# RWKV level loop: every head's intermediates in the opposite partition half, update and score products taken in turn with others

## The chip, the core and the metric

One core of one Trainium2 chip runs the whole program. The metric is the time of one execution on the device in microseconds (us); lower is better.

## What is computed

One step of a two-layer encoder for 320 frames (a prompt of 256, which are 4 chunks of 64, and a sample of 64, chunk 4). The first layer mixes the frames by an RWKV-7 recurrence with 8 heads of 64 in parallel to gated linear attention (GLA) with 4 heads, then a dense SwiGLU. The second has HGRN2 and a top-2-of-8 expert SwiGLU. The change lies in the RWKV part:

```python
def rwkv7_recurrence(r, w, k, v, kk, a, s0):
    def step(s, inp):
        r_t, w_t, k_t, v_t, kk_t, a_t = inp
        sa = jnp.einsum('bhvk,bhk->bhv', s, kk_t)
        s = (s * w_t[:, :, None, :] - sa[..., None] * (kk_t * a_t)[:, :, None, :]
             + v_t[..., None] * k_t[:, :, None, :])
        return s, jnp.einsum('bhvk,bhk->bhv', s, r_t)
```

The kernel computes it by chunks of 64 frames: for each chunk and head it inverts a triangular 64x64 matrix of frame products, and then carries the 64x64 states from chunk to chunk.

## The kernel before, in words

A pair of heads shares the 128 partitions: one in partitions 0 to 63 (half 0), one in 64 to 127 (half 1); `par` is the half, `f` the pair (0 to 3), written f = 2i + e. A product of one head and one chunk is a 64x64 by 64x64 matmul in float32. It reads both operands from one half and may write to either half of PSUM, so it uses one of four corners of TensorE's array: two **straight** ones (half 0 to 0, 1 to 1) and two **crossing** ones (0 to 1, 1 to 0). The trace shows each product as two MATMUL records, so 5 chunks x 8 heads x 2 = 80 records for a product over all of them.

`turned_pairs` (product in L712) issues the products of a list of chunks: pairs with e = 0 straight, pairs with e = 1 moved by its arguments `from_` and `to`, which say whether the odd heads' operands and result lie in the other half. With 0, 1 or 1, 0 two straight products alternate with two crossing ones. With 1, 1 all are straight. `diag` (L696) is straight always. The places, in the order of the program on TensorE (PE):

- `grams` (from L836): frame products of the chunks; kind "t" (three groups of 2, 2 and 1 chunks, 32, 32 and 16 records) by `turned_pairs` 0, 1; the others straight (L696, L856).
- `tm` transposes, GLA values and keys (L696, L772, L856).
- The level loop, `pe.Fori(1, LEVELS)`, 5 rounds over one body. `HALVES` splits the 5 chunks in two groups, [0, 1, 2] and [3, 4]. A round is X = At x Tm (L902, `turned_pairs` 0, 1) for both groups, then the GLA level's 20 straight score products (`level_scores`, L734), then for each group Y = Tt x Xm (L912; 1, 0) and Yt = Xm x Tt (L918; 1, 1). Round 0's Tm and Tt come from the grams.
  VectorE (DVE) multiplies X by a mask into Xm (L1731), copies the scores by mask (L1612) and makes the next level's GLA operand (L1644, L1645, L1639). ScalarE (ACT) copies Y to Tm (L2638) and Yt to Tt (L2640), and makes GLA exponentials (L2561, L2562). PE waits for the Xm of a group ahead of its Y (`inv_x`), for the scores' copy ahead of group 1's Yt, which is written into the same banks 6 and 7 (`gla_sc`), for the copy of Y ahead of the next X (`inv_y`), and for that of Yt of group 1 ahead of the scores (`inv_ready`).
- The steps, [0, 4], [1], [2], [3]: PE makes W1 (`w1`) from G1 and the carried state, last scores (step 0 alone, L761), the outputs' first two parts (`bo`), then U = Tt x W1, then TK x V (L696) into the state update `dh`, then the next step's W1 from G1. It waits for ACT's copy of U (L2659) and adds TQ x U to `dh` (`each`, L696) and G2 x U to the output. DVE copies W1 (L1765) ahead of U, and updates the state (L1784, L1785) behind `dh`; the next step waits for it. All but the L696 ones go by `turned_pairs` (L712).
- `rows_back` (L991): the output's rows by a product with the identity, odd f crossing, then GLA outputs (L805), ACT and DVE copies and the dense products of the output projection (L609, L613).

```python
                a_, z_ = par ^ (e & from_), par ^ (e & to)
                src, dst = slice(64 * a_, 64 * a_ + 64), slice(64 * z_, 64 * z_ + 64)
```

The remaining time (dense and expert SwiGLU) is dense float32 products split in two parts; the change doesn't touch it.

Of the kernel before, what the change touches and what calls it, by code (L numbers as in the profile page):

```python
# [75 lines left out]
def mixed_trunk(nc, ins, outs):  # L76
    ctx = ExitStack()
    with ctx:
# [154 lines left out]

        HALVES = [[0, 1, 2], [3, 4]]
        LAST = LEVELS - 1
# [317 lines left out]
        def _(pe):  # L553
# [138 lines left out]
            def diag(b, col, left, right, start, stop):  # L692
# [5 lines left out]
                return mm  # L698

            def turned_pairs(two, chunks, left, right, from_, to, start, stop):  # L700

                for j, c in enumerate(chunks):
                    for i in range(RF // 2):
                        for e in range(2):
                            l_, r_ = left(c, 2 * i + e), right(c, 2 * i + e)
                            if l_ is None:
                                continue
                            for turn_ in range(2):
                                par = turn_ ^ (e & from_ & to)
                                a_, z_ = par ^ (e & from_), par ^ (e & to)  # L710
                                src, dst = slice(64 * a_, 64 * a_ + 64), slice(64 * z_, 64 * z_ + 64)
                                mm = pe.matmul(two[dst, e, (2 * j + i) * C:(2 * j + i + 1) * C], l_[src], r_[src],  # L712
                                               start=start and j == 0 and i == 0, stop=stop and c == chunks[-1] and i == 1,
                                               skip_group_check=True)
                return mm
# [11 lines left out]

            def level_scores(two):

                for m_ in range(2 * NCH):  # L730
                    c, f = m_ // 2, m_ % 2
                    for par in range(2):
                        rows = slice(64 * par, 64 * par + 64)
                        mm = pe.matmul(two[rows, m_ // NCH, m_ % NCH * C:m_ % NCH * C + C], gla["Z"][rows, f, chunk(c)],  # L734
                                       gla["Z"][rows, f, chunk(c)], start=m_ % NCH == 0, stop=m_ % NCH == NCH - 1,
                                       skip_group_check=True)
                return mm

# [155 lines left out]
            def waited():  # L894

                pe.sem_inc(S("level_waited"), 1)

            with pe.Fori(1, LEVELS) as lv:
                for g, chunks in enumerate(HALVES):
                    pe.wait_ge(S("inv_y"), level_count(lv - 1, g))  # L900
                    waited()
                    turned_pairs(where["X", 1, g], chunks, lambda c, f: At[:, c, f, :], lambda c, f: Tm[:, c, f, :],  # L902
                                 0, 1, True, True).then_inc(S("inv_full"), 1)
                pe.wait_ge(S("inv_ready"), level_count(lv - 1, len(HALVES) - 1))
                pe.wait_ge(*at_count("gla_z", lv + 1))
                waited()
                pe.wait_ge(*first_done)
                level_scores(where["gla_sc", 1]).then_inc(S("gla_sc_full"), 1)
                for g, chunks in enumerate(HALVES):
                    pe.wait_ge(S("inv_x"), level_count(lv - 1, g))  # L910
                    waited()
                    turned_pairs(where["Y", 1, g], chunks, inverse_at, product_at, 1, 0, True, True).then_inc(S("inv_full"), 1)  # L912
                    if g == len(HALVES) - 1:
                        pe.wait_ge(*at_count("gla_sc", lv + 2))
                        waited()
                    else:
                        pe.wait_ge(*grams_done)
                    turned_pairs(where["Yt", 1, g], chunks, product_at, inverse_at, 1, 1, True, True).then_inc(S("inv_full"), 1)  # L918
            for g in range(len(HALVES)):
                for k in YT_AT[g]:  # L920
                    owner[k] = ("inv_ready", level_count(LAST, g))

            pe.wait_ge(*at_count("h_init", 1))
# [26 lines left out]
            for i, step in enumerate(STEPS):  # L950
# [23 lines left out]
                else:  # L974
                    gla_keys(w1_at)
                pe.wait_ge(*at_count("u_done", i + 1))
                each(dh, step, lambda c, f: TQ[:, c, f, :], lambda c, f: U[:, PLACE[c], f, :], False, True).then_inc(S("seq_full"), 1)
                turned_pairs(bo, step, lambda c, f: G2[:, c, f, :], lambda c, f: U[:, PLACE[c], f, :], 0, 1, False, True)\
                    .then_inc(S("seq_full"), 1)
            gla_updates()  # L980
# [2283 lines left out]
```

## Time and profile before

| | |
|---|---|
| time, median of 3 runs | 1468.73 us (1468.45 to 1468.87) |
| time of the profiled execution | 1469.37 us |
| its span | 1467.7 us |
| granted clock of TensorE, mean | 0.995 |
| busy PE, DVE, ACT | 97%, 80%, 65% |
| chain that ended last, by engine | PE 88%, DVE 7%, ACT 3% |
| stretch that the change touches | about 120 to 208 us |

The table is to be read from below: the change lies in one twentieth of the span, all of it in stretches at full granted clock, and the rest follows in the same order.

### The profile page before, as it was taken

What the parts mean: (1) busy time and instruction counts of PE and PEld (TensorE: products, weight loads), DVE (VectorE), ACT (ScalarE), POOL (GpSimd) and SP (SyncE); (2) the same over time, 40 slices, a digit from 0 to 9 for tenths busy, and PEclk for the clock granted to TensorE, in tenths of its full rate; (3) what the DMA queues carried; (4) which work ended last, traced back from release to release, by engine and by line L of the source; (5) the groups of instructions that cost most, each with busy time, mean ns of one, the idle gap of its engine ahead of it and who ended that gap; (6) DMA issues with size and microseconds to landing.
All of it is one profiled execution on the core that took longest, in us unless ns stands there. A gap on an engine that the chain in (4) does not pass through costs nothing.

```text
span 1467.7 us, 29198 instructions
## 1 busy us (share of the span) xinstructions
PE 1428.1 (97%) x11253; PEld 1278.1 (87%) x11254; DVE 1173.1 (80%) x1580; ACT 950.7 (65%) x1257; POOL 76.3 (5%) x152
## 2 busy tenths in 40 slices
PE   7999989999999999999999999999999999999997
PEld 7999988999999899888788888888888888888884
DVE  5686579545535789867998998899988999898997
ACT  4465455433323696476778787778777887877873
POOL 8300000000000000000000000000000000000000
PEclk9999999999999999999999999999999999999999
DMA  8431004544445262217999999999999999999992
GB/s 261 152 106 37 2 15 145 173 144 145 150 143 164 88 187 88 88 59 285 339 390 397 402 394 398 347 396 380 371 397 350 407 379 362 397 353 410 390 345 93
DMA packets 162214, 371.62 MB, mean 253 GB/s; under 512 B 10232, under 2 KB 85968, under 8 KB 162128
## 3 DMA queue, kind: packets, MB, share of 16 engines
q1 hardware_dynamic: 159352, 361.18, 67.2%
q0 software_dynamic: 2160, 7.87, 2.0%
q8 instruction: 61, 1.00, 0.3%
q10 hardware_dynamic: 616, 1.37, 0.2%
q14 instruction: 25, 0.20, 0.0%
HBM read 360.68 MB, written 9.71 MB: 252 GB/s over the span
## 4 chain that ended last, share of the span: by engine, by line
PE 88%; DVE 7%; ACT 3%; issue 1%; DMA 1%; SPq 0%; DVEq 0%; ACTq 0%
PE psum L1371 11%; PE psum L1372 11%; PE psum L1373 11%; PE psum L596 10%; PE psum L598 9%; PE psum L597 9%; PE psum L1395 5%; PE psum L1397 5%; PE psum L1396 5%; PE psum L712 2%; PE psum L1380 1%; PE psum L696 1%; PE psum L1133 1%; DVE wd_lo L1468 1%; PE psum L609 1%
## 5 line engine op out<-in xcount | busy, mean ns | idle before, releaser
L2184 DVE TENSOR_TENSOR w_lo<-moe_ring,w_hi 128x1024 fp32r<-128x1024 f32 (+1 forms) x560 | 608.3, 1155 | 28.9 <-ACT w_hi L2916 28.9
L2916 ACT ACTIVATE w_hi<-moe_ring 128x1024 fp32r<-128x1024 f32 (+1 forms) x560 | 531.6, 1015 | 69.4 <-PE psum L1397 39.0
L1371 PE MATMUL psum<-w_hi,xe_hi 128*128 128x512 f32 (+1 forms) x768 | 288.1, 375 | 1.6 <-DVE w_lo L2184 1.4
L1372 PE MATMUL psum<-w_hi,xe_lo 128*128 128x512 f32 (+1 forms) x768 | 285.9, 372 | 0.0
L1373 PE MATMUL psum<-w_lo,xe_hi 128*128 128x512 f32 (+1 forms) x768 | 285.4, 372 | 0.0
L1468 DVE TENSOR_TENSOR wd_lo<-arena,wd_hi 128x1024 fp32r<-128x1024 f32 x141 | 169.9, 1208 | 132.9 <-ACT wd_hi L2441 132.6
L596 PE MATMUL psum<-in_hi,wd_hi 128*128 128x320 f32 x800 | 250.5, 313 | 2.5 <-DVE wd_lo L1468 1.2
L2441 ACT ACTIVATE wd_hi<-arena 128x1024 fp32r<-128x1024 f32 (+1 forms) x140 | 146.2, 1047 | 157.4 <-PE psum L598 151.8
L598 PE MATMUL psum<-in_hi,wd_lo 128*128 128x320 f32 x800 | 247.2, 309 | 0.0
L597 PE MATMUL psum<-in_lo,wd_hi 128*128 128x320 f32 x800 | 247.1, 309 | 0.0
L1371 PEld LDWEIGHTS psum<-w_hi,xe_hi 128*128 128x128 f32 x768 | 144.5, 188 | 28.4 <-DVE w_lo L2184 2.9
L1373 PEld LDWEIGHTS psum<-w_lo,xe_hi 128*128 128x128 f32 x768 | 144.2, 188 | 25.8
L1372 PEld LDWEIGHTS psum<-w_hi,xe_lo 128*128 128x128 f32 x768 | 144.5, 188 | 24.9
L596 PEld LDWEIGHTS psum<-in_hi,wd_hi 128*128 128x128 f32 x800 | 150.1, 188 | 5.7 <-issue 1.8
L597 PEld LDWEIGHTS psum<-in_lo,wd_hi 128*128 128x128 f32 x800 | 150.2, 188 | 0.4
L598 PEld LDWEIGHTS psum<-in_hi,wd_lo 128*128 128x128 f32 x800 | 150.2, 188 | 0.0
L1395 PE MATMUL psum<-w_hi,gt_hi 128*128 128x512 f32 x256 | 101.3, 396 | 0.2 <-DVE w_lo L2184 0.2
L1397 PE MATMUL psum<-w_lo,gt_hi 128*128 128x512 f32 x256 | 99.7, 389 | 0.0
L1396 PE MATMUL psum<-w_hi,gt_lo 128*128 128x512 f32 x256 | 99.7, 389 | 0.0
L596 PE MATMUL psum<-hid_hi,wd_hi 128*128 128x320 f32 x224 | 69.7, 311 | 1.3 <-DVE wd_lo L1468 1.3
L598 PE MATMUL psum<-hid_hi,wd_lo 128*128 128x320 f32 x224 | 69.1, 309 | 0.0
L597 PE MATMUL psum<-hid_lo,wd_hi 128*128 128x320 f32 x224 | 69.1, 309 | 0.0
(449 smaller groups left out, 1799.5 us busy)
## 6 DMA issues: line engine op xcount, KB each, us to landing
moe_ring<-in_moe_w SPq DMA_DIRECT2D x216, 1024.0 KB, 8.8
moe_ring<-in_moe_w SPq DMA_DIRECT2D x64, 768.0 KB, 5.7
arena<-in_ffn_w SPq DMA_DIRECT2D x30, 1024.0 KB, 5.3
arena<-in_w_in_c SPq DMA_DIRECT2D x16, 1024.0 KB, 5.5
arena<-in_w_in_ab SPq DMA_DIRECT2D x12, 1024.0 KB, 5.5
arena<-in_w_out_ab SPq DMA_DIRECT2D x4, 1024.0 KB, 5.1
arena<-in_w_out_c SPq DMA_DIRECT2D x4, 1024.0 KB, 5.0
arena<-in_ffn_w SPq DMA_DIRECT2D x4, 768.0 KB, 4.3
```

Source lines behind the costliest of these rows:

```text
L596: pe.matmul(b[:, 0:T], w_[0][:, cols], x_hi, start=start, stop=False)
L597: pe.matmul(b[:, 0:T], w_[0][:, cols], x_lo, start=False, stop=False)
L598: return pe.matmul(b[:, 0:T], w_[1][:, cols], x_hi, start=False, stop=stop)
L1371: pe.matmul(b[:, 0:w], xe_hi[:, k, :], hi_[:, c0:c1], start=(k == 0), stop=False)
L1372: pe.matmul(b[:, 0:w], xe_lo[:, k, :], hi_[:, c0:c1], start=False, stop=False)
L1373: mm = pe.matmul(b[:, 0:w], xe_hi[:, k, :], lo_[:, c0:c1], start=False, stop=(k == KC - 1))
L1395: pe.matmul(E_Y[half][:, :], g_hi[:, g], hi_[:, cols], start=first, stop=False)
L1396: pe.matmul(E_Y[half][:, :], g_lo[:, g], hi_[:, cols], start=False, stop=False)
L1397: mm = pe.matmul(E_Y[half][:, :], g_hi[:, g], lo_[:, cols], start=False, stop=final)
L1468: dve.tensor_tensor(wd_lo[:, m_ % DENSE_UNITS, 0:words], src, rounded_of(m_)[:, 0:words], ALU.subtract).then_inc(S("dense_lo"), 1)
L2184: dve.tensor_tensor(w_lo[:, i % UNITS, 0:unit_words(i)], moe_unit(i), w_hi[:, i % UNITS, 0:unit_words(i)], ALU.subtract)\
L2916: act.activation(w_hi[:, i % UNITS, 0:unit_words(i)], moe_unit(i), ACT.Copy).then_inc(S("e_hi"), 1)
```

## The change

`turned` is now one product, and with `from_` or `to` 1 the operands or the result lie in the other half for every head, not the odd ones alone. So a product with 0, 1 or 1, 0 is all crossing, one with 1, 1 all straight. Groups of the levels are [0, 1] and [2, 3, 4].

In the level body X of group 0 and the first half of X of group 1 stand alone; then PE waits for `inv_ready` and `gla_z`, and the other 12 products of group 1 are taken in turn with the 20 scores: 2 crossing, then 2 or 4 scores. Y and Yt of a group are taken in turn, 2 and 2; so the wait for the scores' copy stands ahead of group 1's Y too. In the steps the product TQ x U and G2 x U are taken in turn, one and one. The rest of the steps, "t" of the grams and `rows_back` keep their place and turn all crossing.

```diff
-        HALVES = [[0, 1, 2], [3, 4]]
+        HALVES = [[0, 1], [2, 3, 4]]
...
+            def turned(two, chunks, head, left, right, from_, to, start=True, stop=True):
+
+                j, c, i, e, par = head
+                a_, z_ = par ^ from_, par ^ to
+                src, dst = slice(64 * a_, 64 * a_ + 64), slice(64 * z_, 64 * z_ + 64)
+                return pe.matmul(two[dst, e, (2 * j + i) * C:(2 * j + i + 1) * C], left(c, 2 * i + e)[src], right(c, 2 * i + e)[src],
+                                 start=start and j == 0 and i == 0, stop=stop and c == chunks[-1] and i == 1, skip_group_check=True)
...
+                heads, scored = chunk_heads(HALVES[1]), 0
+                alone = len(heads) // 2
+                for head in heads[:alone]:
+                    turned(where["X", 1, 1], HALVES[1], head, product_of, before_at, 0, 1)
                 pe.wait_ge(S("inv_ready"), level_count(lv - 1, len(HALVES) - 1))
...
+                for n, head in enumerate(heads[alone:]):
+                    mm = turned(where["X", 1, 1], HALVES[1], head, product_of, before_at, 0, 1)
+                    if n == alone - 1:
+                        mm.then_inc(S("inv_full"), 1)
+                    if n % 2:
+                        until = 2 * ((n + 1) * scores // (2 * alone))
+                        for m_ in range(scored, until):
+                            score = level_score(where["gla_sc", 1], m_)
+                        scored = until
+                score.then_inc(S("gla_sc_full"), 1)
                 for g, chunks in enumerate(HALVES):
                     pe.wait_ge(S("inv_x"), level_count(lv - 1, g))
                     waited()
-                    turned_pairs(where["Y", 1, g], chunks, inverse_at, product_at, 1, 0, True, True).then_inc(S("inv_full"), 1)
                     if g == len(HALVES) - 1:
                         pe.wait_ge(*at_count("gla_sc", lv + 2))
...
+                    for head, other in zip(heads[::2], heads[1::2]):
+                        for h_ in (head, other):
+                            y = turned(where["Y", 1, g], chunks, h_, inverse_at, product_at, 1, 0)
+                        if other == heads[-1]:
+                            y.then_inc(S("inv_full"), 1)
+                        for h_ in (head, other):
+                            yt = turned(where["Yt", 1, g], chunks, h_, product_at, inverse_at, 1, 1)
...
-                each(dh, step, lambda c, f: TQ[:, c, f, :], lambda c, f: U[:, PLACE[c], f, :], False, True).then_inc(S("seq_full"), 1)
-                turned_pairs(bo, step, lambda c, f: G2[:, c, f, :], lambda c, f: U[:, PLACE[c], f, :], 0, 1, False, True)\
-                    .then_inc(S("seq_full"), 1)
+                for head in chunk_heads(step):
+                    j, c, i_, e, par = head
+                    f, rows = 2 * i_ + e, slice(64 * par, 64 * par + 64)
+                    o = (RF * j + f) * C
+                    state = pe.matmul(dh[rows, o:o + C], TQ[rows, c, f, :], U[rows, PLACE[c], f, :], start=False,
+                                      stop=c == step[-1] and f == RF - 1, skip_group_check=True)
+                    if head == chunk_heads(step)[-1]:
+                        state.then_inc(S("seq_full"), 1)
+                    out = turned(bo, step, head, lambda c, f: G2[:, c, f, :], lambda c, f: U[:, PLACE[c], f, :], 0, 1, False, True)
...
-                            a_ = par ^ (f % 2)
+                            a_ = par ^ 1
```

On PE, the body of the level loop, before: L712 are the products of X (24 and 16), of Y and Yt (64, 16), L734 the scores.

```order
L898 ISA
L712 MATMUL psum<-arena 64x64 x24
L900 REGISTER_ALU
L712 MATMUL psum<-arena 64x64 x16
L905 REGISTER_ALU
L734 MATMUL psum<-arena 64x64 x20
L712 MATMUL psum<-arena 64x64 x64
L914 REGISTER_ALU
L712 MATMUL psum<-arena 64x64 x16
```

The same body now: L709 are the products of `turned`, L736 the scores. L913 stands at the wait for `gla_z`, L930 at that for the scores' copy.

```order
L709 MATMUL psum<-arena 64x64 x16
L905 REGISTER_ALU
L709 MATMUL psum<-arena 64x64 x12
L913 REGISTER_ALU
L709 MATMUL psum<-arena 64x64 x2
L736 MATMUL psum<-arena 64x64 x2
L709 MATMUL psum<-arena 64x64 x2
L736 MATMUL psum<-arena 64x64 x4
...
L736 MATMUL psum<-arena 64x64 x4
L709 MATMUL psum<-arena 64x64 x32
L930 REGISTER_ALU
L709 MATMUL psum<-arena 64x64 x48
```

The counts are the same, 120 and 20. X has moved into the scores, group 1 has 48 products behind the wait for the scores' copy where 16 stood behind it, and group 0 has 32 ahead of it.

On PE, the end of step 1, before (L696 are TK x V and TQ x U, the first L712 the next step's W1, the last G2 x U and what follows):

```order
L712 MATMUL psum<-arena 64x64 x48
L696 MATMUL psum<-arena 64x64 x8
L712 MATMUL psum<-arena 64x64 x8
L696 MATMUL psum<-arena 64x64 x8
L712 MATMUL psum<-arena 64x64 x40
```

And now (L1007 is TQ x U):

```order
L709 MATMUL psum<-arena 64x64 x33
L696 MATMUL psum<-arena 64x64 x8
L709 MATMUL psum<-arena 64x64 x8
L1007 MATMUL psum<-arena 64x64
L709 MATMUL psum<-arena 64x64
L1007 MATMUL psum<-arena 64x64
L709 MATMUL psum<-arena 64x64
L1007 MATMUL psum<-arena 64x64
```

The 8 products TQ x U no longer stand ahead of the 8 of G2 x U, but alternate with them; W1, output and U products keep their place and number.

## Rows read from the trace of the kernel before

**Rows 1.** The page: busy time, and the chain that ended last.

```profile
PE 1428.1 (97%) x11253; PEld 1278.1 (87%) x11254; DVE 1173.1 (80%) x1580; ACT 950.7 (65%) x1257; POOL 76.3 (5%) x152
...
PE 88%; DVE 7%; ACT 3%; issue 1%; DMA 1%; SPq 0%; DVEq 0%; ACTq 0%
```

**Rows 2.** The chain in order of time, 126 to 196 us: start, us, what.

```profile
126.70 0.14 issue
126.84 0.69 PE psum L712 x32
...
129.66 8.70 PE psum L696 x296
...
150.10 0.71 issue
...
180.00 0.39 issue
...
190.65 0.95 DVE stat L1738
```

**Rows 3.** Timeline, PE: start, us, group, [idle before <-releaser].

```profile
126.84 0.69 PE L712 MATMUL psum<-arena 64*64 64x64 f32 x32 [0.54 <-DVE arena L1705]
...
129.96 7.21 PE L696 MATMUL psum<-ident,arena 64*64 64x64 f32 x240
...
186.84 0.93 PE L712 MATMUL psum<-arena 64*64 64x64 f32 x48 [0.75 <-DVE arena L1785]
```

**Rows 4.** Timeline of the third and fourth rounds, all engines.

```profile
160.34 4.92 PE L712 MATMUL psum<-arena 64*64 64x64 f32 x238
...
161.31 0.81 ACT L2638 ACTIVATE arena<-psum 128x768 f32<-128x768 f32 x1 [1.80 <-PE psum L712]
...
162.67 0.81 ACT L2640 ACTIVATE arena<-psum 128x768 f32<-128x768 f32 x1 [0.56 <-PE psum L712]
...
164.07 0.60 ACT L2640 ACTIVATE arena<-psum 128x512 f32<-128x512 f32 x1
...
164.85 1.55 DVE L1731 TENSOR_TENSOR arena<-psum,lower 128x768 f32<-128x768 f32 x2 [2.06 <-PE psum L712]
...
165.05 1.30 PE L734 MATMUL psum<-arena 64*64 64x64 f32 x38
...
166.22 4.92 PE L712 MATMUL psum<-arena 64*64 64x64 f32 x238
...
166.45 0.56 DVE L1612 COPY_PREDICATED arena<-upper,psum 128x160 f32<-128x160 int32 x2
```

**Rows 5.** DVE timeline, first round's copy of the scores.

```profile
147.59 0.89 DVE L1612 COPY_PREDICATED arena<-upper,psum 128x160 f32<-128x160 int32 x2
```

**Rows 6.** Groups by shape, 144.8 to 177.6 us: busy us, mean ns.

```profile
L1731 DVE TENSOR_TENSOR arena<-psum,lower 128x768 f32<-128x768 f32 x5 | 4.8, 958 | 9.0 <-PE psum L712 9.0
...
L1731 DVE TENSOR_TENSOR arena<-psum,lower 128x512 f32<-128x512 f32 x5 | 3.4, 680 | 0.0
L1639 DVE TENSOR_TENSOR arena<-arena 128x640 f32<-128x640 f32 x4 | 3.3, 824 | 0.1
L2638 ACT ACTIVATE arena<-psum 128x768 f32<-128x768 f32 x4 | 3.2, 811 | 11.9 <-PE psum L712 11.9
```

**Rows 7.** Timeline, steps 1 and 2 and the head of step 3.

```profile
182.85 1.80 PE L712 MATMUL psum<-arena 64*64 64x64 f32 x63 [0.85 <-DVE arena L1785]
...
183.92 0.58 PEld L712 LDWEIGHTS psum<-arena 64*64 64x64 f32 x15 [0.29 <-DVE arena L1765]
...
185.18 0.62 PE L696 MATMUL psum<-arena 64*64 64x64 f32 x14
```

**Rows 8.** Timeline, step 2: U, TK x V, TQ x U.

```profile
187.92 0.55 PE L712 MATMUL psum<-arena 64*64 64x64 f32 x14
...
188.21 0.27 PE L696 MATMUL psum<-arena 64*64 64x64 f32 x2
188.25 0.28 PE L712 MATMUL psum<-arena 64*64 64x64 f32 x2
...
189.00 0.62 PE L696 MATMUL psum<-arena 64*64 64x64 f32 x14
```

**Rows 9.** Timeline, `rows_back` and the GLA outputs behind it.

```profile
197.93 0.96 PE L991 MATMUL psum<-ident,arena 64*64 64x64 f32 x46
...
198.82 2.45 PE L805 MATMUL psum<-arena 64*128 64x64 f32 x40
...
201.20 0.69 PE L991 MATMUL psum<-ident,arena 64*64 64x64 f32 x32
```

More of the change, by code:

```diff
@@ L698, in diag, with chunk_heads @@
                 return mm
-            def turned_pairs(two, chunks, left, right, from_, to, start, stop):
[L702 to L714, printed above, removed]
+            def chunk_heads(chunks):
+                return [(j, c, i, e, par) for j, c in enumerate(chunks) for i in range(RF // 2) for e in range(2) for par in range(2)]
+            def turned(two, chunks, head, left, right, from_, to, start=True, stop=True):
[4 more added lines that the diff above has]
+                                 start=start and j == 0 and i == 0, stop=stop and c == chunks[-1] and i == 1, skip_group_check=True)
+            def turned_pairs(two, chunks, left, right, from_, to, start, stop):
+                for head in chunk_heads(chunks):
+                    _, c, i, e, _ = head
+                    if left(c, 2 * i + e) is not None and right(c, 2 * i + e) is not None:
+                        mm = turned(two, chunks, head, left, right, from_, to, start, stop)
                 return mm
@@ L726, in _, with level_score @@
                   .then_inc(S("gate_full"), 1)
[L728 to L737, printed above, removed]
+            def level_score(two, n):
+                m_, par = n // 2, n % 2
+                c, f = m_ // 2, m_ % 2
+                rows = slice(64 * par, 64 * par + 64)
+                return pe.matmul(two[rows, m_ // NCH, m_ % NCH * C:m_ % NCH * C + C], gla["Z"][rows, f, chunk(c)],
+                                 gla["Z"][rows, f, chunk(c)], start=m_ % NCH == 0, stop=m_ % NCH == NCH - 1, skip_group_check=True)
             def first_scores():
@@ L896, in waited @@
                 pe.sem_inc(S("level_waited"), 1)
+            product_of = lambda c, f: At[:, c, f, :]
+            before_at = lambda c, f: Tm[:, c, f, :]
+            scores = 4 * NCH
             with pe.Fori(1, LEVELS) as lv:
[L899 to L903, printed above, removed]
+                pe.wait_ge(S("inv_y"), level_count(lv - 1, 0))
+                waited()
+                turned_pairs(where["X", 1, 0], HALVES[0], product_of, before_at, 0, 1, True, True).then_inc(S("inv_full"), 1)
+                pe.wait_ge(S("inv_y"), level_count(lv - 1, 1))
+                waited()
+                heads, scored = chunk_heads(HALVES[1]), 0
+                alone = len(heads) // 2
+                for head in heads[:alone]:
+                    turned(where["X", 1, 1], HALVES[1], head, product_of, before_at, 0, 1)
                 pe.wait_ge(S("inv_ready"), level_count(lv - 1, len(HALVES) - 1))
+                waited()
                 pe.wait_ge(*at_count("gla_z", lv + 1))
@@ L907, in _ @@
                 pe.wait_ge(*first_done)
-                level_scores(where["gla_sc", 1]).then_inc(S("gla_sc_full"), 1)
+                for n, head in enumerate(heads[alone:]):
[8 more added lines that the diff above has]
+                score.then_inc(S("gla_sc_full"), 1)
                 for g, chunks in enumerate(HALVES):
@@ L917, in _ @@
                         pe.wait_ge(*grams_done)
-                    turned_pairs(where["Yt", 1, g], chunks, product_at, inverse_at, 1, 1, True, True).then_inc(S("inv_full"), 1)
+                    heads = chunk_heads(chunks)
+                    for head, other in zip(heads[::2], heads[1::2]):
[5 more added lines that the diff above has]
+                            yt = turned(where["Yt", 1, g], chunks, h_, product_at, inverse_at, 1, 1)
+                    yt.then_inc(S("inv_full"), 1)
             for g in range(len(HALVES)):
@@ L921, in _ @@
                     owner[k] = ("inv_ready", level_count(LAST, g))
+            for k in Y_AT[0]:
+                owner[k] = ("inv_full", inverse_count("Y", LAST, 0))
             pe.wait_ge(*at_count("h_init", 1))
@@ L976, in _ @@
                 pe.wait_ge(*at_count("u_done", i + 1))
-                each(dh, step, lambda c, f: TQ[:, c, f, :], lambda c, f: U[:, PLACE[c], f, :], False, True).then_inc(S("seq_full"), 1)
-                turned_pairs(bo, step, lambda c, f: G2[:, c, f, :], lambda c, f: U[:, PLACE[c], f, :], 0, 1, False, True)\
-                    .then_inc(S("seq_full"), 1)
+                for head in chunk_heads(step):
[7 more added lines that the diff above has]
+                    out = turned(bo, step, head, lambda c, f: G2[:, c, f, :], lambda c, f: U[:, PLACE[c], f, :], 0, 1, False, True)
+                out.then_inc(S("seq_full"), 1)
             gla_updates()
```

## The prediction

> **What bounds the kernel now.** I read the page first. TensorE is busy 97% of the span, and the chain that ended last runs over PE for 88% of it [rows 1]. So time that PE gains or loses on that chain goes to the end. The chain in order of time [rows 2] shows where: from 126.84 to 181 us it is PE almost alone, interrupted by two pieces of "issue", 0.71 us at 150.10 and 0.39 at 180.00, where PE waits for nothing that the trace names. From there the steps alternate between PE, DVE and ACT, and from 195.8 PE carries it again. So most of the touched stretch has no slack, and the question is how fast PE gets through these small products.
>
> Next, how fast each kind of product is. 240 records of straight products take 7.21 us with the last one's own 0.22 in it: 6.99 / 239 = **29.2 ns each** [rows 3]. 48 records of `turned_pairs` 0, 1, two straight and two crossing in turn, take 0.93: 0.71 / 47 = **15.1 ns each** [rows 3]. The size is the same, so it is the corners: four in use go twice as fast as two. A second reading within one round says the same. Between ACT's start on Y of group 0 (161.31) and on its Yt (162.67) lie 48 straight records, 1.36 us; between its start on Yt of group 1 (164.07) and DVE's on X (164.85) lie 48 mixed ones, 0.78 [rows 4]. No stretch of before has crossing products alone. They use two corners, one per half, as the straight ones do. From below they can't beat 15.1, which four corners need, from above nothing is known. I take 29.2, since a corner in the mixed stretch (a record each 4 x 15.1 = 60 ns) and one in the straight stretch (2 x 29.2 = 58) have the same speed of their own: the number of corners in use decides.
>
> Per 16 records (one chunk) a product that turns from mixed to crossing alone costs 16 x 14.1 ns = 0.23 us, if PE is on the chain there.
>
> **The levels.** PE's own time of a round now: X and Y mixed, 160 x 15.1 = 2.42; Yt and scores straight, 120 x 29.2 = 3.50; sum 5.92. The trace has 166.22 - 160.34 = 5.88 [rows 4], so nothing but PE limits a round. After the change: X of group 0 alone 32 x 29.2 = 0.93; half of X of group 1 24 x 29.2 = 0.70; the rest with the scores, where the 40 straight score records on two corners last longest, 1.17; Y and Yt in turn, 160 x 15.1 = 2.42. Sum 5.22, a gain of **0.66 to 0.7 a round**, 3.4 in five.
>
> Against it stand the waits, which were covered before and now are not. PE may begin Y and Yt of group 1 only when the scores are copied. Behind the end of X of group 1 come the mask product over three chunks, 0.96 [rows 6], and the two score copies, 0.57 (0.90 in the first two rounds) [rows 4, 5], and about 0.05 of signals: 1.55 us (1.85). PE has work for 1.1 in that time: the last scores, some 0.15 past the signal, and Y and Yt of group 0, 64 x 15.1 = 0.97. It **waits 0.45 (0.8)**. Second, X of group 1 needs ACT's copy of Y of three chunks, 0.81 [rows 6] and about 0.25 of signals, against 0.93 of X of group 0: 0.14 more in four rounds. So a round is 5.22 + 0.45 + 0.14 = 5.8 (three times) and 6.15 (twice): -0.2 and +0.5. **Levels: +0.2 us**, from -3.4 (waits hidden) to +1.4 (X ends only with the scores). The next operand's chain on DVE (L1644, L1645, L1639 0.82 [rows 6]) starts behind the copies and has over 2 us; I cost it at nothing. The 0.71 of issue stands in the first round [rows 2] and I leave it.
>
> How far X of group 1 ends ahead of the scores rests on products overtaking each other. The trace shows it: two L696 records start at 188.21, the two L712 records that stand ahead of them in the program at 188.25 and after [rows 8]; corners have queues of their own. The Trainium skill (TensorE: Matmul & The Clock Gate, The mechanism) says otherwise, that matmuls start and end strictly in program order. By it X would end some 0.1 us later in each round, and the levels come to +0.7; the trace decides here.
>
> **Grams "t".** 32 records of the second group and 16 of the third turn crossing on the chain: +0.68. The first group's 32 lie ahead of 0.54 us in which PE waits for DVE [rows 3], which hides their 0.45. **+0.7.**
>
> **Step 0** is PE's alone: W1 32 + 16, output 32 + 16, U 32, next W1 16: 144 records x 14.1 = 2.03. Where a crossing batch meets a straight one they overlap by a record or two per corner; I take **+1.9**. The taking in turn of TQ x U and G2 x U brings nothing: 32 straight records alone last 0.93, 64 mixed 0.97, and DVE waits for the end of the straight ones either way. Against this, the issue at 180.00 (0.39) is time from fetching; with PE slower in front of it, it should go: **-0.4**, from 0.
>
> **Steps 1 and 2.** From the state's arrival to U PE needs 1.07 (182.85 to 183.92 [rows 7]): W1, DVE's copy, and in its shade the output's parts. Now W1 and both parts are 48 crossing records, 1.40, which outlasts W1 and its copy (0.5 + 0.23 + 0.53 = 1.26): +0.33 each. From U to TQ x U it took 1.26 (to 185.18 [rows 7]) and 1.08 (187.92 to 189.00 [rows 8]). Now 48 records, U, TK x V and W1, 1.40 less some 0.15 of overlap: 1.25, so 0 and +0.17. **+0.8**, from +0.5 to +1.5.
>
> **Step 3.** DVE's normalization, which starts at 190.65 with the state of step 2 [rows 2], holds the chain until 194.9, and PE's 0.5 of delay fits nearly into it: **+0.1**, up to +0.5.
>
> **rows_back.** 48 records took 0.75 to 0.86, now 1.40; 32 took 0.69 with 0.22 of tail, now 0.93 without it [rows 9]; PE's GLA outputs follow at once: +0.54 and +0.46, **+1.0**, from +0.5.
>
> Sum: 0.2 + 0.7 + 1.9 - 0.4 + 0.8 + 0.1 + 1.0 = **+4.3 us**. The profiled execution took 1469.37; with it 1473.7. The median of the runs is 0.64 lower, so the forecast is **1473.0 us**, 0.3% slower. In short: the level loop's gain is eaten by its waits, while all products that lost their straight neighbours pay in full.
>
> **Rivals.** (a) The forecast, with its own range of 1470.5 to 1475.5: 0.55.
> (b) The waits of the levels are hidden, and the whole 3.4 is gained. For it speaks that DVE is idle 9.0 us ahead of L1731 [rows 6]; against it that this idleness lies elsewhere in the round. 1473.0 - 3.6 = 1469.4, no change: 0.17.
> (c) The update products hinder each other. Now each TQ product is followed by a G2 product from the same half, in the order 0-0, 0-1, 1-1, 1-0, an order that no row of before has. If two products from one half don't overlap, 64 records cost 29.2 rather than 15.1 ns, and the state comes at their end: 0.9 in step 0, 0.45 in each of steps 1 and 2, up to 0.5 in step 3: +2.3, 1475.3, slower: 0.19. Against it: the mixed batches have four corners, hence two of one half, at work at once. The Trainium skill (same page and section) has a rule for it: a weight load overlaps with running matmuls only where the row group differs, by which these neighbours would lose the overlap.
> (d) The other side. Crossing products alone run at 15.1, so no product pays and X costs 0.47 and 0.35 instead of 0.93 and 0.70. Then all terms but the levels' are 0, and the levels need 4.4 a round plus waits: nearly the whole difference turns into waits if the copies are the limit (-0.5), none if they are covered (-7.5). It decides from half of that on: about -4, 1464.7, faster: 0.09. Against it speaks the equal speed of a corner in both kinds of batch.
>
> **How the numbers follow.** A measurement of this kernel can tell about 0.2%, 2.9 us, from no change. Slower by more: most of (a), 0.46, and (c), 0.19: 0.65. Within: the rest of (a) and (b): 0.26. Faster: (d), 0.09. The range leaves out (d) and takes in (b) below, and above the sum of (c) and the upper ends of two or three terms: 1468.8 to 1478.0.
>
> **What would show it.** In the changed kernel's trace: crossing batches alone at 29 ns a record (X of group 0: 32 records in 0.93 plus tail); Y and Yt in turn at 15; PE idle 0.4 to 0.8 us a round ahead of Y of group 1, released by DVE's L1612; rounds of 5.8 and 6.1 us; step 0 longer by 1.5 to 2; "issue" at its end gone; steps 1 and 2 of 4.3 us each; L991's 48 and 32 records at 29 ns each. The forecast falls if a crossing batch goes at 15 ns, if rounds take 5.2, or if PE isn't what the steps wait for.

## The result, and the profile after

| | before | after |
|---|---|---|
| median of the runs, us | 1468.66 (11 runs, 1468.19 to 1470.67) | 1472.66 (11 runs, 1470.96 to 1474.27) |
| profiled execution, its own time | 1469.37 | 1472.96 |
| its span | 1467.7 | 1471.2 |

The ratio is **1.0029, 95% interval 1.0021 to 1.0037**: slower by 4.0 us of the medians. The forecast was 1473.0 and "slower". The total came out within 0.4 us, but its terms did not: the levels were forecast too low, the grams and step 0 too high, and these errors nearly cancel.

The page of after answers to [rows 1]. Nothing in it tells of the change: PE is the bound as before, with the same share of the chain.

```profile
PE 1428.6 (97%) x11253; PEld 1278.3 (87%) x11254; DVE 1173.0 (80%) x1580; ACT 950.2 (65%) x1257; POOL 75.8 (5%) x152
...
PE 88%; DVE 7%; ACT 3%; issue 1%; DMA 1%; SPq 0%; DVEq 0%; ACTq 0%
```

So I cut the touched stretch into stages by marks that both kernels have: PE's start on the first L856 record (121.18 before, 120.74 after), DVE's start on the fifth product with the mask of G1 (145.26, 144.79), ACT's start on the last copy of Yt (175.83, 177.02), PE's start after each state update, and PE's start on L613 behind the outputs (207.77, 211.33). This is the view by windows; first before, then after:

```profile
core 0: us, PE busy (x) PEld busy (x) DVE busy (x) ACT busy (x) POOL busy (x), PEclk, DMA share, GB/s
121.18:145.26 24.08, 23.54 (x659) 23.07 (x662) 17.01 (x37) 13.47 (x26) 0.00 (x0) 1.00 0.02 4
145.26:175.83 30.57, 29.86 (x1414) 29.71 (x1408) 19.86 (x36) 14.62 (x26) 0.00 (x0) 1.00 0.00 1
175.83:207.77 31.94, 26.40 (x893) 24.33 (x883) 21.56 (x46) 14.80 (x31) 0.00 (x0) 1.00 0.02 4
```

```profile
120.74:144.79 24.05, 23.43 (x657) 22.97 (x658) 17.02 (x36) 13.48 (x26) 0.00 (x0) 1.00 0.02 4
144.79:177.02 32.23, 28.29 (x1397) 27.08 (x1395) 19.83 (x36) 13.86 (x25) 0.00 (x0) 1.00 0.00 1
177.02:211.33 34.31, 28.78 (x897) 27.36 (x894) 21.67 (x46) 14.92 (x31) 0.00 (x0) 1.00 0.01 3
```

The three stages together last 86.59 us before and 90.59 after. That is 4.0, as much as the medians differ. The spans of these two executions differ by 3.5, because the part ahead of the stretch happens to be 0.44 shorter in the second; behind the stretch they agree within 0.1. So no loss lies outside the stretch. The granted clock is 1.00 in all six rows. The middle pair is the interesting one. In the levels PE was busy 1.57 us less (29.86 to 28.29), as the change intends, and yet the stage is 1.66 longer (30.57 to 32.23): PE was idle for 0.71 of it, and is now for 3.94: 3.03 of it ahead of Y of group 1 and 0.90 of "issue". In the third stage PE has simply more to do, 2.38, and the stage is 2.37 longer.

**The levels.** Timeline of after: PE's starts on Y of group 1 in the first two rounds, then the third and fourth rounds on all engines; [rows 4] stood for these before.

```profile
149.00 1.11 PE L709 MATMUL psum<-arena 64*64 64x64 f32 x58 [0.79 <-DVE arena L1645]
...
156.21 3.83 PE L709 MATMUL psum<-arena 64*64 64x64 f32 x154 [0.79 <-DVE arena L1645]
...
162.57 3.83 PE L709 MATMUL psum<-arena 64*64 64x64 f32 x154 [0.48 <-DVE arena L1645]
...
167.31 1.15 PE L709 MATMUL psum<-arena 64*64 64x64 f32 x59
...
167.37 0.96 DVE L1764 TENSOR_TENSOR arena<-psum,lower 128x768 f32<-128x768 f32 x1 [1.15 <-PE psum L709]
168.25 0.55 DVE L1645 COPY_PREDICATED arena<-upper,psum 128x160 f32<-128x160 int32 x2
...
168.94 1.63 PE L709 MATMUL psum<-arena 64*64 64x64 f32 x96 [0.49 <-DVE arena L1645]
170.59 0.81 ACT L2671 ACTIVATE arena<-psum 128x768 f32<-128x768 f32 x1 [1.08 <-PE psum L709]
...
170.76 2.01 PE L709 MATMUL psum<-arena 64*64 64x64 f32 x58 [0.19 <-issue]
```

Each round has two holes. The first is the forecast one: at 167.37 X of group 1 is done and DVE takes the mask product over three chunks (L1764, 0.96), then the two copies of the scores (L1645, 0.55), and PE starts Y of group 1 at 168.94, 1.57 later. It has the 59 records at 167.31 to do in that time, whose last starts at 168.24. So PE starts nothing for 0.70 us, of which 0.49 shows as idle behind the last record's end. In the first two rounds, where the copies take 0.86, it starts nothing for 1.01, of which 0.79 shows as idle. The second hole was not in the forecast. Between the 96 records of Y and Yt and the next round's X lie 0.19 of "issue", 0.15 to 0.17 in the other rounds; PE waits for nothing that the trace shows. It lies where the loop's body ends and begins anew: the loop's turn. There 0.36 to 0.41 lies between two starts.

By DVE's starts on X of group 1 (161.00 and 167.37) this round lasts 6.37, the next one too. It was 5.88, and 5.8 was forecast. The first two last 7.21 and 6.67, where 6.15 was forecast; before they took 7.10 and 5.88.

**The rates.** The first row is a crossing batch alone, the row at 168.94 above Y and Yt in turn:

```profile
126.39 0.97 PE L709 MATMUL psum<-arena 64*64 64x64 f32 x26 [0.62 <-DVE arena L1738]
127.15 0.27 PE L696 MATMUL psum<-arena 64*64 64x64 f32 x2
127.17 0.28 PE L709 MATMUL psum<-arena 64*64 64x64 f32 x3
```

(0.97 - 0.22) / 25 = 30 ns a record, and (1.63 - 0.22) / 95 = 14.8 ns. Both are what the corners said, 29.2 and 15.1 [rows 3]. These rows also show records of the later straight batch (L696) starting at 127.15, before the crossing ones ahead of them in the program (127.17) have all begun, as in [rows 8]. The batch at 126.39 has 32 records, 0.93 us at 29.2 ns, and the next one begins after 0.76: **a join of a crossing and a straight batch hides 0.17 us**.

**The steps and the outputs**, chain of waits in order of time; [rows 2, 7] were the steps before, [rows 9] the outputs.

```profile
184.89 1.91 PE psum L709 x58
...
189.15 1.91 PE psum L709 x58
...
193.40 1.91 PE psum L709 x58
...
200.94 1.06 PE psum L1024 x37
202.00 2.38 PE psum L805 x40
204.38 1.08 PE psum L1024 x32
```

At the head of each step the chain now runs for 1.91 us over crossing records without a break: W1, both parts of the outputs and U. Before, it ran over W1 alone (16 records, 0.51) and DVE's copy, and the outputs stood beside it. Steps 1 and 2 last 4.25 each (184.89, 189.15, 193.40). In `rows_back` (L1024) the chain holds 1.06 and 1.08 where it held 0.74 and 0.62 on L991, the same line before.

All stages, after and in the experiments below (us, from the same marks):

| | grams | levels | step 0 | step 1 | step 2 | step 3 | outputs | sum |
|---|---|---|---|---|---|---|---|---|
| before | 24.07 | 30.57 | 7.02 | 3.99 | 3.83 | 5.13 | 11.97 | 86.59 |
| after | 24.05 | 32.23 | 7.87 | 4.25 | 4.25 | 5.17 | 12.75 | 90.59 |
| e1_groups | 24.05 | 29.32 | 7.87 | 4.25 | 4.25 | 5.17 | 12.75 | 87.66 |
| e2_y_apart | 24.05 | 34.46 | 7.81 | 4.25 | 4.25 | 5.17 | 12.75 | 92.76 |
| e3_scores_apart | 24.05 | 31.50 | 7.87 | 4.25 | 4.25 | 5.17 | 12.75 | 89.84 |
| e4_update_apart | 24.05 | 32.01 | 7.92 | 4.24 | 4.23 | 5.17 | 12.75 | 90.37 |
| e5_out_mixed | 24.05 | 32.02 | 7.53 | 4.11 | 4.11 | 5.13 | 11.97 | 88.92 |
| e6_groups_mixed | 24.05 | 29.36 | 7.72 | 4.11 | 4.10 | 5.13 | 11.97 | 86.43 |
| e7_early_scores | 24.05 | 29.65 | 7.71 | 4.11 | 4.11 | 5.13 | 11.97 | 86.73 |
| e8_pairs | 24.04 | 29.29 | 7.19 | 4.11 | 4.11 | 5.13 | 11.98 | 85.85 |
| e9_turn | 24.05 | 30.04 | 6.99 | 4.11 | 4.11 | 5.13 | 11.97 | 86.39 |

Stages that an edit doesn't touch repeat within 0.05 us, except "levels" and "step 0", where pieces of "issue" differ (by 0.2 in the levels of after against e4 and e5). Each row is one execution. The time of a whole run is coarser: the stretch itself begins anywhere from 119.3 to 121.5 us in these executions. So the stages carry the reading, and the ratio of the runs is its check.

### The profile page after: what moved, and what is told of

The parts are those of the page before. It is cut to its first block, busy times and chain, and to the rows that moved or that the text cites. A ratio compares the mean times of both kernels' runs of the same rounds, so it can differ in the third digit from the quotient of the medians.

```text
span 1471.2 us, 29204 instructions
## 1 busy us (share of the span) xinstructions
PE 1428.6 (97%) x11253; PEld 1278.3 (87%) x11254; DVE 1173.0 (80%) x1580; ACT 950.2 (65%) x1257; POOL 75.8 (5%) x152
## 3 DMA queue, kind: packets, MB, share of 16 engines
q0 software_dynamic: 2160, 7.87, 2.0%
## 4 chain that ended last, share of the span: by engine, by line
PE 88%; DVE 7%; ACT 3%; issue 1%; DMA 1%; SPq 0%; DVEq 0%; ACTq 0%
PE psum L1404 11%; PE psum L1405 11%; PE psum L1406 11%; PE psum L596 9%; PE psum L597 9%; PE psum L598 9%; PE psum L1428 5%; PE psum L1430 5%; PE psum L1429 5%; PE psum L709 2%; PE psum L1413 1%; PE psum L1166 1%; DVE wd_lo L1501 1%; PE psum L696 1%; PE psum L609 1%
```

## Experiments

Each edit is to the changed kernel or to the experiment named. A ratio is to the kernel before, run on the same chip, whose median was 1468.16 for e1 to e4, 1468.20 for e5 to e7 and 1467.79 for e8 and e9.

### e1_groups: three and two chunks again

```diff
-        HALVES = [[0, 1], [2, 3, 4]]
+        HALVES = [[0, 1, 2], [3, 4]]
```

> The changed kernel with the old groups, [0, 1, 2] and [3, 4]. Theory A (the waits of the levels eat their gain: after X of group 1 the mask product and the scores' copy take longer than PE has work): the mask product of group 1 shrinks from 0.96 to 0.68 us and Y with Yt of group 0 grow from 64 to 96 records, 0.97 to 1.45 us, so the wait ahead of Y of group 1 (PE idle 0.48 to 0.79 us a round in the changed kernel) disappears and a round falls from 6.37 to about 5.7 us; the kernel becomes 3 to 4 us faster than the changed one, about level with the kernel before. Rival B (the exposed time is the loop's own turn and the products' rate, whatever the groups): rounds stay at 6.2 or more, gain under 1 us.

Measured: 1471.26 us, ratio 1.0013 (1.0004 to 1.0022). The levels went from 32.23 to 29.32, the later rounds from 6.37 to 5.84, nothing else moved. By the ratios the kernel is some 2.3 us faster than the changed one, not 3 to 4, and by the interval not quite level with the kernel before: rounds of 5.7 were expected, and the loop's turn makes the difference. The chain of waits holds no DVE piece any more, only that turn:

```profile
160.11 2.51 PE psum L709 x156
162.62 0.15 issue
162.77 2.02 PE psum L709 x62
...
165.95 2.48 PE psum L709 x156
168.43 0.15 issue
```

With group 0 of three chunks PE has 96 records, 1.4 us, to do while the scores are copied, and the mask product ahead of the copies is one of two chunks. With the old groups the wait is hidden.

The stage of 29.32 is 1.25 us below before's 30.57, but little of this lies in the repeated rounds: they last 5.87, 5.84 and 5.81 against 5.88. By DVE's starts on X of group 1 the stage begins 0.84 slower, the first round is 0.57 shorter, the other three 0.12 together, and what stands behind the last X 1.40 shorter. There, in the last round, Y and Yt in turn gain over 1 us, and no turn follows. In a repeated round 0.47 less of PE's work (80 x 14.1 = 1.13 gained by Y and Yt, 64 x 14.1 = 0.90 lost by X alone, 16 x 15.1 = 0.24 gained by X among the scores) stands against 0.33 for the turn. So even with the wait hidden a round gains next to nothing.

### e2_y_apart: Y, then Yt

```diff
+                    turned_pairs(where["Y", 1, g], ..., 1, 0, True, True).then_inc(S("inv_full"), 1)
...
-                    for head, other in zip(heads[::2], heads[1::2]):
...
+                    turned_pairs(where["Yt", 1, g], ..., 1, 1, True, True).then_inc(S("inv_full"), 1)
```

The edit does two things: Y of group 1 also stands ahead of the wait for the scores' copy again, as before the change.

> The changed kernel, Y and Yt of a group one after the other again. PE's own time of a round grows by 160 x 14.1 ns = 2.3 us if a crossing batch and a straight batch next to each other don't overlap; theory A with overlapping joins (about 0.23 us hidden at each change between crossing and straight, two products per corner in the queue): four joins hide up to 0.9 and the two waits (0.7 and 0.36 us a round) are covered, so a round is about 6.4 to 6.8 us and the kernel 0 to 2 us slower than the changed one. Without overlap at the joins: 7.3 us a round, 4 to 5 us slower.

Measured: 1474.39 us, ratio 1.0036 (1.0024 to 1.0048). The levels take 34.46, 2.2 more than after, and behind the first round (0.49 of "issue") PE has no idle piece in the levels:

```profile
160.56 5.89 PE L709 MATMUL psum<-arena 64*64 64x64 f32 x209
...
167.40 5.83 PE L709 MATMUL psum<-arena 64*64 64x64 f32 x209
```

A round by these two starts is 6.84. Worked out at 29.2 ns for every record but those with the scores it would be X 0.93 + 0.70, scores 1.17, Y and Yt 160 x 29.2 = 4.67, together 7.47. The starts of single records in the trace show where the missing 0.63 lies. In a round there are four places at which some 12 records start 15 ns apart instead of 29: from the scores to Y, from Y to Yt, from Yt to Y, from Y to Yt (160.4, 161.1, 161.9 and 163.1 us). Each hides 0.17, 0.68 together: the later batch begins before the earlier one has started all its records, as at 127.15 above. The fifth place, the loop's turn from Yt to X at 164.4, hides nothing; its 16 records take 0.09 more than 16 x 29.2 ns. Together 7.47 - 0.68 + 0.09 = 6.88.

So the turn no longer shows as idle, but it isn't free: against a join inside the body it costs 0.26.

### e3_scores_apart: X alone, then the scores

```diff
-                    if n % 2:
-                        until = 2 * ((n + 1) * scores // (2 * alone))
-                        for m_ in range(scored, until):
-                            score = level_score(where["gla_sc", 1], m_)
-                        scored = until
+                for m_ in range(scores):
+                    score = level_score(where["gla_sc", 1], m_)
```

> The changed kernel, X of group 1 whole and then the scores. If the wait for the scores' copy (counted from the end of X of group 1) sets the round, X ends 1 us earlier in the round's order and PE's extra 24 records x 29.2 = 0.70 us replace the wait of 0.70: rounds stay at 6.3 to 6.4 us and the time within 0.5 us of the changed kernel's. If PE's own work sets it: 0.7 us more a round, 3.5 us slower.

Measured: 1472.36 us, ratio 1.0024 (1.0015 to 1.0034). Rounds of 6.31 against 6.37, and 6.73 and 6.54 in the first two against 7.21 and 6.67. Taking X and the scores in turn saves PE 0.7 a round and gains nothing here: X of group 1 ends earlier in e3, the copies are done in time, and PE idles 0.14 in two rounds and not at all in the others. What was won by the turns was given back as the wait, and a little more: the levels of 31.50 are 0.5 shorter than the 32.01 and 32.02 of e4 and e5, whose level body is that of after. The sum agrees: X 2.34 + scores 1.17 + Y and Yt 2.42 + the turn 0.36 = 6.29.

### e4_update_apart: TQ x U, then G2 x U

```diff
-                for head in chunk_heads(step):
...
-                    out = turned(bo, step, head, ..., 0, 1, False, True)
-                out.then_inc(S("seq_full"), 1)
+                each(dh, step, ..., False, True).then_inc(S("seq_full"), 1)
+                turned_pairs(bo, step, ..., 0, 1, False, True).then_inc(S("seq_full"), 1)
```

> The changed kernel, TQ x U whole and then G2 x U. My account: the alternation neither gains nor costs on the chain, since DVE waits for the last TQ product either way (16 straight records 0.47 us, 32 mixed 0.48): steps 1 and 2 stay at 4.25 us each, the time within 0.5 us of the changed kernel's. Rival (neighbours from one half hinder each other): steps shorter by 0.2 to 0.45 us each, 0.9 in step 0, 1 to 2 us faster.

Measured: 1471.52 us, ratio 1.0020 (1.0010 to 1.0029). The steps don't change, 4.23 and 4.24 by the chain of waits:

```profile
185.37 1.91 PE psum L709 x58
...
189.60 1.91 PE psum L709 x58
...
193.84 1.91 PE psum L709 x58
```

In step 0 of after the records of TQ x U and G2 x U in turn start 15 ns apart (182.4 to 183.3 us), the rate of four corners. The ratio of whole runs is 0.0009 lower than after's, 1.3 us, more than the 0.5 expected and within what rival (c) would give; but the two intervals overlap, and the stretch is only 0.22 shorter, all of it in the levels. So neighbours from the same row half don't hinder each other here, and taking these two in turn brings nothing either.

### e5_out_mixed: the outputs' products mixed again

```diff
+            def mixed_pairs(two, chunks, left, right, from_, to, start, stop):
...
+                        mm = turned(two, chunks, head, left, right, e & from_, e & to, start, stop)
...
-                turned_pairs(bo, step, lambda c, f: G1[:, c, f, 1, :], values, 0, 1, True, False)
-                turned_pairs(bo, step, inputs(1), carried, 0, 1, False, False)
+                mixed_pairs(bo, step, lambda c, f: G1[:, c, f, 1, :], values, 0, 1, True, False)
+                mixed_pairs(bo, step, inputs(1), carried, 0, 1, False, False)
...
-                            a_ = par ^ 1
+                            a_ = par ^ (f % 2)
```

G2 x U is mixed too and stands behind TQ x U, as in e4.

> The changed kernel with the outputs' products (bo) and rows_back two straight, two crossing in turn as before, and G2 x U behind TQ x U. Theory A: crossing batches alone cost 14 ns more a record wherever PE is on the chain, less about 0.15 us at each join with a straight batch. rows_back falls by 0.8 us (10.33 back to 9.55), step 0 by 0.3 to 0.6 us (48 output records), steps 1 and 2 by 0.1 each (W1 alone crossing, its copy ends later than the output's parts again); levels, grams and step 3 unchanged. Sum 1.3 to 1.6 us less than the changed kernel from the grams to the output projection. Rival: the later stages wait for DVE or ACT, and PE's time there doesn't count: under 0.3 us.

Measured: 1471.52 us, ratio 1.0023 (1.0013 to 1.0032). The stretch is 1.67 shorter than after's: outputs -0.78 (back to before's 11.97), step 0 -0.34, steps 1 and 2 -0.14 each, step 3 -0.04, and 0.2 in the levels, where nothing was edited. Without those 0.2 it is 1.46, within the 1.3 to 1.6 expected. `rows_back` is on the chain as it was before:

```profile
199.25 0.74 PE psum L1024 x43
200.00 2.38 PE psum L813 x40
202.37 0.62 PE psum L1024 x32
```

### e6_groups_mixed: e1 and e5 together

The edits are those of e1 and e5.

> Both e1_groups (levels 28.6 us) and e5_out_mixed (outputs and rows_back mixed). If the two parts of the loss add up: 86.9 - 2.9 - 1.4 = 82.6 us from the first gram to the output projection, against 82.9 in the kernel before: the time within 0.1% of before. If they hide one another: 83.5 or more.

Measured: 1468.49 us, ratio 1.0002 (0.9993 to 1.0011). The stretch takes 86.43 against 86.59 before: -4.16 from after's 90.59, where e1 alone gave -2.93 and e5 alone -1.67. The 0.44 by which the sum is larger lies in the levels and step 0, where the pieces of "issue" differ; every other stage adds up. Together the two parts make up the loss of the change. Against before, the levels are 1.2 better in e6, and steps 0, 1 and 2, where W1 and U still cross, are 0.70, 0.12 and 0.27 worse.

### e7_early_scores: e6 with 4 products of X alone

```diff
-                alone = len(heads) // 2
+                alone = 4
+                taken = len(heads) - alone
...
```

> e6_groups_mixed with 4 instead of 8 products of X of group 1 alone ahead of the scores, the other 12 in turn with them. PE's own time of a round falls by 8 records x 29.2 = 0.23 us, if the copy of Yt of group 1 (inv_ready) has come by then, which the margin allows narrowly: rounds 5.6 us, levels 1.0 to 1.2 us less than e6, kernel 1 us faster than before, about 1467. If inv_ready comes later, PE idles there and the gain is under 0.3 us.

Measured: 1468.86 us, ratio 1.0003 (0.9994 to 1.0012). Rounds of 5.64 to 5.75 against 5.81 to 5.86, some -0.1 where -0.23 was expected; why so little stays open. The levels are longer in all, 29.65 against 29.36. That comes from the first round, chain of waits:

```profile
149.46 0.65 PE psum L709 x26
150.10 1.44 issue
151.54 0.81 PE psum L709 x38
```

The "issue" in the first round of the loop is 1.44 here, 0.71 before [rows 2] and 0.24 after; in e4 and e5 it leaves no idle time, only 0.25 between two starts. Where it shows it comes at the same place, 118 to 123 records behind the scores, the first time that the body is run through, and only there. What it is was not tried by itself, and why its size differs so much is open.

### e8_pairs: e6 with the steps' crossing products beside straight ones

```diff
-                turned_pairs(u, step, ..., 1, 0, True, True).then_inc(S("seq_full"), 1)
-                each(dh, step, lambda c, f: TK[:, c, f, :], values, True, False)
+                in_turn([... update_value(h_) for h_ in chunk_heads(step)], [... key_value(h_) for h_ in chunk_heads(step)])
```

`in_turn` issues two of the first list and two of the second. U goes with TK x V, and in step 0 W1 with the last scores, so that W1 also waits for their operand (`gla_z`).

> e6_groups_mixed, and in the steps crossing batches taken in turn with straight ones that don't depend on them: W1 of step 0 (48 crossing records) with the last scores (40 straight), U with TK x V. Theory A (crossing and straight use different corners, and the time is that of the longer): step 0 falls by 0.5 to 1.2 us from 7.69 (40 x 29.2 = 1.17 and 32 x 29.2 = 0.93 no longer stand by themselves, less the joins they had), steps 1 and 2 by 0.1 from 4.11, the sum from the first gram to the output projection from 82.8 to about 81.6; the kernel about 1 us faster than before. Rival (the rate is one of dispatch, and any batch of different lines costs the same in turn as apart): step 0 unchanged.

Measured: 1467.26 us, ratio 0.9996 (0.9987 to 1.0005). Step 0 fell by 0.53, from 7.72 to 7.19, although a piece of "issue" of 0.73 stands in it now, where e6 has 0.13:

```profile
179.09 0.27 PE L709 MATMUL psum<-arena 64*64 64x64 f32 x1 [0.73 <-issue]
```

Steps 1 and 2 stayed at 4.11, where 0.1 less each was expected:

```profile
181.56 0.71 PE psum L709 x19
182.36 0.43 DVE arena L1835
182.84 0.27 PE psum L709 x2
...
183.53 0.45 PE psum L709 x16
184.00 0.62 PE psum L696 x14
...
184.73 0.43 DVE arena L1854
185.19 0.44 DVE arena L1855
185.67 0.71 PE psum L709 x19
```

Here the chain alternates between engines: W1, DVE's copy, U, the next batch, two DVE operations. From U's start to DVE's on the state it is 1.89 us in e8 (182.84 to 184.73) and 1.89 in e5 (184.83 to 186.72), so the faster batch of U and TK x V gained nothing there. ACT's copy of U, which TQ x U waits for, shows why; e8, then e5:

```profile
183.56 0.38 ACT L2729 ACTIVATE arena<-psum 128x256 f32<-128x256 f32 x1 [2.18 <-PE psum L709]
```

```profile
185.56 0.39 ACT L2692 ACTIVATE arena<-psum 128x256 f32<-128x256 f32 x1 [2.17 <-PE psum L709]
```

It begins 0.72 after U's start in e8 and 0.73 in e5, and TQ x U 0.44 after that in both (184.00, 186.00). U's 16 records among those of TK x V are spread over 32 x 14.8 ns = 0.47 us, as long as they last alone (16 x 29.2 = 0.47). So U's last record comes no sooner, and what PE gains on the rest ends in waiting for that copy. The stretch is 0.74 us shorter than before's, which a whole run doesn't show (the interval reaches over 1).

### e9_turn: e8 with the last chunk's Y and Yt apart

```diff
-                    for head, other in zip(heads[::2], heads[1::2]):
+                    apart = 8 if g == len(HALVES) - 1 else 2
+                    at_once = [heads[n:n + 2] for n in range(0, len(heads) - apart, 2)] + [heads[len(heads) - apart:]]
```

So the body ends with 8 straight products, 16 records, alone.

> e8_pairs with Y and Yt of chunk 4 one after the other, chunk 3 still in turn. In rounds that end with products in turn PE idles 0.15 us at the loop's turn; where Yt alone (29 ns a record) ends the round, it doesn't. If the idling comes from the turn meeting a batch at full rate, with nothing left in the queue, it vanishes here and pays for the 16 x 14.1 = 0.23 us that the chunk costs apart (less a join): rounds within 0.1 us of e8's. If it is a wait of X for something else, it stays and rounds are 0.1 to 0.2 us longer.

Measured: 1467.40 us, ratio 1.0000 (0.9991 to 1.0009). Rounds of 5.87 to 5.92 against 5.81 to 5.87 in e8, within the 0.1 expected, and PE runs through the turn:

```profile
158.58 4.92 PE L709 MATMUL psum<-arena 64*64 64x64 f32 x217
...
164.45 4.91 PE L709 MATMUL psum<-arena 64*64 64x64 f32 x217
```

The price of taking 32 records out of the turns is 32 x 14.1 ns = 0.45. The loop's turn pays back 0.33 (0.36 from the last start to the next one, less the spacing of 0.03), a join of Y and Yt hides 0.15, and the first 8 records behind the turn take 0.11 more than 8 x 29.2 ns. Together 5.82 + 0.45 - 0.33 - 0.15 + 0.11 = 5.90. The levels as a whole are 0.75 longer than in e8, which the rounds explain in part only: 0.34 lies in the first one and 0.25 behind the last X.

This, with e2, settles the second hole: it shows when a batch on four corners ends the body, and not when one on two corners does, though about 0.1 us is lost then too. Why is not shown.

## Why the prediction was right, and where it wasn't

| term | forecast | measured | shown by |
|---|---|---|---|
| grams | +0.7 | 0.0 | stages |
| levels | +0.2 | +1.66 | stages, e1, e2, e9 |
| step 0, with the fetching | +1.5 | +0.85 | stages, e8 |
| steps 1 and 2 | +0.8 | +0.68 | stages, e5 |
| step 3 | +0.1 | +0.04 | stages |
| outputs | +1.0 | +0.78 | stages, e5 |
| sum | +4.3 | +4.0 | |

**Right.** "The number of corners in use decides": crossing products alone go at 30 ns, a straight and a crossing one in turn at 14.8. With that rival (d) fell. That the gain of the level loop would be eaten by PE's wait for the copy of the scores, at the place named (0.79, 0.79, 0.48, 0.49, 0.48 of idle ahead of Y of group 1 in the five rounds) was right as a mechanism: e1 takes away the wait, and with it 2.9 us. Rival (b) fell: the wait was not hidden, and where it is hidden, in e1, the levels gain 1.25 against before, not 3.4. e4 takes away the neighbours of rival (c), and nothing happens. The steps came out at 4.25 for the forecast 4.3, and the "issue" of 0.39 at 180.00 [rows 2] is gone from after's chain. That it was fetching, no run shows.

**Wrong in the levels, step "It waits 0.45 (0.8)".** The 1.55 us from X's end to PE's restart (the three terms named add up to 1.58) was right: it was 1.57. The 1.1 us of work that PE would have in it was too much. It was 0.87: Y and Yt of group 0 began among the last scores, ahead of X's end, so part of the cover had been used already. This is 0.25 in the later rounds and 0.21 in the first two, 1.01 against 0.8, by the same overtaking that I had counted in favour of the change. The Trainium skill (TensorE: Matmul & The Clock Gate, The mechanism), by which starts are strictly in program order, gave +0.7 for the levels. That is closer to the 1.66 than my +0.2, but the rows at 127.15 don't agree with its reason.

**Wrong in the levels, what was left out.** The loop's turn, 0.36 from the last start to the next one between rounds, had no term. In the kernel before a straight batch on two corners ended the body, and its later rounds show no gap of 0.1 us or more between two starts. The change put a batch on four corners there. With both corrections a round comes to 5.22 + 0.70 + 0.36 = 6.28 of the measured 6.37. The 0.14 for X of group 1 behind ACT's copy of Y did not come there. But 56 records behind the turn, where the program waits for `inv_ready` and `gla_z`, 0.11 to 0.15 lies between two starts, about the 0.09 that is missing; which of the two it waits for was not settled. Over the whole stage the corrections add up to about 1.9 where the forecast was off by 1.46: 1.17 for the waits, 1.3 for four turns, 0.4 for these gaps, -0.56 for the term of 0.14 and -0.47 for the "issue" of the first round, which I had left as it was. The rest of 0.4 stays open.

**Wrong in the grams and in step 0, "they overlap by a record or two per corner".** A join hides 0.17 us, some six records in all (rows at 127.15, e2). I had priced a batch by its length alone. On a short batch, 16 or 32 records, the joins are half of the surcharge or more. In the grams the second crossing batch costs 0.19 instead of 0.45 (from its start to the next L856 record 1.74, before 1.55). Behind it the way to the transposes is 0.19 shorter than before (1.38 against 1.57), where +0.23 was forecast; so all of the 0.7 vanished. Step 0 has four joins, seen as groups of records that start 15 ns apart (at 178.1, 179.1, 181.3 and 182.0): 2.03 - 4 x 0.17 - 0.39 for the "issue" that is gone is 0.96 by this estimate, of the measured 0.85, where 1.5 was forecast.

So 1.5 us too little in the levels stood against 0.7 too much in the grams, 0.65 in step 0 and 0.4 elsewhere. The total was near by luck: errors of opposite sign, most of them from how batches meet.

## What to carry to other kernels

When small products move between corners of the array, count for each batch the corners that it uses (here 29 to 30 ns a record on two, 15 on four), then look at its neighbours: a join of a straight and a crossing batch hides 0.17 us, and what ends a loop's body decides whether its turn shows. Before shortening work that covers a wait, write down what runs during the wait and for how long; here 0.7 us a round saved on X and the scores came back as the wait and gained nothing (e3). Larger work behind the wait's start, with a shorter mask product ahead of the copies, took the wait away and shortened the round (e1). Versions with the old groups and with the outputs left mixed undo the loss (e6 to e9), but none is measurably faster than the kernel before.

## What the runs showed of the chip that I had not expected

- The loop's turn on PE: 0.15 us idle and 0.36 between starts when four corners are busy at its end; no idle, but about 0.1 us over the usual spacing, when two are (e2, e9 against e6).
- Where a crossing and a straight batch meet, some 12 records pass at the rate of four corners, which hides 0.17 us (after at 127.15, e2).
- Two adjacent products that read the same row half and write different column halves keep the full rate, 15 ns a record (e4 against after: steps of 4.24 and 4.25).
- The gap of "issue" in the first round of the loop is 0 to 1.44 us over these kernels, larger than most of the effects studied here. Each was read from one execution, so how much of this is the edits' doing is open; it differs for e4 too (0, after 0.24), whose edit lies outside the loop.
